# A chunked linear recurrence on TensorE: transposes in place of identity products, one addend moved to VectorE, and a merged product

## What is computed

```python
def wkv7_scan(state, inputs, reverse):
    def step(S, xs):
        r, w, k, v, a, b = xs
        sa = jnp.einsum('bhvk,bhk->bhv', S, a)
        S = S * w[:, :, None, :] + sa[..., None] * b[:, :, None, :] + v[..., None] * k[:, :, None, :]
        return S, jnp.einsum('bhvk,bhk->bhv', S, r)
    ...
# before it:  kk = kk * lax.rsqrt(jnp.sum(jnp.square(kk), -1, keepdims=True) + 1e-12)
# after it:   var = jnp.mean(jnp.square(y - mu), -1, keepdims=True)
#             yn = (y - mu) * lax.rsqrt(var + GN_EPS)
```

## Time and profile before

| | |
|---|---|
| time, median of 3 | 3914.93 us (3911.76 to 3934.26) |
| span of the profiled execution | 3915.0 us |
| TensorE busy | 3610.4 us, 92% |
| VectorE / ScalarE / GpSimd busy | 2019.5 / 1544.0 / 251.1 us |
| mean granted TensorE clock | 0.965 |

### The profile page before, as it was taken

How to read it: one execution, slowest core, us unless ns; L and a number is a source line. 1 busy time by engine, 2 the same in 40 slices (tenths; PEclk the granted TensorE clock), 3 DMA queues, 4 the chain that set the end, 5 groups by cost and what they waited for, 6 DMA issues and landing times. The chain is left out here.

```text
span 3915.0 us, 73945 instructions
## 1 busy us (share of the span) xinstructions
PE 3610.4 (92%) x32796; PEld 2969.4 (76%) x32796; DVE 2019.5 (52%) x3476; ACT 1544.0 (39%) x2599; POOL 251.1 (6%) x295
## 2 busy tenths in 40 slices
PE   7899999999899998989988799989999999999998
PEld 3577666767666676777678689847989799999877
DVE  1444454544445457675465646666544455555444
ACT  1333343333333333354454444334443444444433
POOL 0001111110111113002000000100000000000000
PEclk8899899999999998999999899999999999999999
DMA  9423333242343315443324454424554545555554
GB/s 365 145 74 96 89 106 104 81 126 70 94 126 91 100 56 192 170 153 106 97 97 138 154 166 143 138 97 140 172 183 140 169 163 183 183 179 189 194 174 160
DMA packets 349484, 548.76 MB, mean 140 GB/s; under 512 B 11724, under 2 KB 119916, under 8 KB 346988
## 3 DMA queue, kind: packets, MB, share of 16 engines
q1 hardware_dynamic: 346716, 538.78, 42.6%
q10 hardware_dynamic: 2448, 5.24, 0.4%
HBM read 535.86 MB, written 8.13 MB: 139 GB/s over the span
## 5 line engine op out<-in xcount | busy, mean ns | idle before, releaser
L302 PE MATMUL lane<-r,r 128*128 128x256 f32 (+1 forms) x8520 | 1504.7, 325 | 48.4 <-DVE r L260 41.7
L302 PE MATMUL bank<-r,r 128*128 128x512 f32 (+2 forms) x6360 | 1403.0, 359 | 37.6 <-DVE r L260 29.0
L302 PEld LDWEIGHTS lane<-r,r 128*128 128x128 f32 x8520 | 1260.6, 190 | 222.2 <-DVE r L260 48.6
L260 DVE TENSOR_TENSOR r<-ring,r 128x1024 fp32r<-128x1024 f32 x770 | 939.6, 1227 | 940.9 <-ACT r L299 939.6
L302 PEld LDWEIGHTS bank<-r,r 128*128 128x128 f32 x6360 | 1045.0, 193 | 253.5 <-issue 55.3
L299 ACT ACTIVATE r<-ring 128x1024 fp32r<-128x1024 f32 x770 | 807.9, 1055 | 967.5 <-PE lane L302 566.7
L302 PE MATMUL lane<-arena 64*64 64x64 f32 (+5 forms) x13708 | 664.2, 250 | 57.1 <-issue 20.4
L302 PEld LDWEIGHTS lane<-arena 64*64 64x64 f32 (+3 forms) x13708 | 504.9, 140 | 203.3 <-issue 121.4
L299 ACT ACTIVATE arena<-lane 128x256 f32<-128x256 f32 (+3 forms) x578 | 252.6, 457 | 567.0 <-PE lane L302 468.0
L271 DVE COPY arena<-lane 128x256 f32<-128x256 f32 (+3 forms) x366 | 131.7, 361 | 303.5 <-PE lane L302 300.5
L260 DVE TENSOR_TENSOR arena<-arena 128x256 f32<-128x256 f32 (+7 forms) x568 | 259.8, 488 | 36.0 <-ACT arena L299 14.8
(11 more groups left out here) (95 smaller groups left out, 1357.5 us busy)
## 6 DMA issues: line engine op xcount, KB each, us to landing
ring<-in_w_gate_up SPq DMA_DIRECT2D x88, 1024.0 KB, 5.1
ring<-in_mod_w SPq DMA_DIRECT2D x73, 1024.0 KB, 5.3
ring<-in_ev_w_in SPq DMA_DIRECT2D x44, 1024.0 KB, 8.7
ring<-in_w_down SPq DMA_DIRECT2D x44, 1024.0 KB, 5.1
ring<-in_od_w_in SPq DMA_DIRECT2D x40, 1024.0 KB, 5.1
ring<-in_w_in SPq DMA_DIRECT2D x40, 1024.0 KB, 5.1
ring<-in_w_xkv SPq DMA_DIRECT2D x32, 1024.0 KB, 5.2
ring<-in_ev_w_out SPq DMA_DIRECT2D x28, 1024.0 KB, 5.1
```

The costliest lines, as they stand in the source:

```text
L260: return Nothing() if self.e is None else self.e.tensor_tensor(o, a, b, op)
L302: return Nothing() if self.e is None else self.e.matmul(o, l, r, start=start, stop=stop)
```

## The change

Three things. `spread` uses `pe.tr` in place of `pe.mm` with the same tile and identity. VectorE also writes I + PT for `c` = 1, in two instructions of 64 partitions after the one for `c` = 0, each reading one half and writing the other. And `double` is written anew: step 0 has no products for T at all, and ScalarE then copies only the parts 0 and 2 of its bank; in steps 1 to 3 the products for PT and T of `c` = 1 are one of 128 columns, as those of `c` = 0; the identity product comes after the product with P and not before.

```diff
     def spread(s, b):
         for c in range(2):
-            i = pe.mm(M.bank[b[0]][:, c * P:c * P + P], s.rs[:, c * P:c * P + P], ident, True, True)
+            i = pe.tr(M.bank[b[0]][:, c * P:c * P + P], s.rs[:, c * P:c * P + P], ident)
         i.then_inc(*pe.n(("full", *b)))
...
             four = [(c, q) for c in range(2) for q in range(2)]
-            for q in range(2):
-                pe.mm(out(1, q, 1, 2), C("i64")[half(q), :], tt(1, q), True, False)
+            both = 0 if 1 <= i <= 3 else 1
             for c, q in four:
-                if c == 0 and 1 <= i <= 3:
-                    o = pe.mm(out(c, q, 0, 2), pm(c, q), cur[half(q), c, h, 0:2, :], True, True)
-                elif i or c:
-                    o = pe.mm(out(c, q, 1, 2), pm(c, q), tt(c, q), c == 0, True)
-            if i < 4:
-                for c, q in four[0 if i == 0 else 2:]:
+                if i:
+                    o = pe.mm(out(c, q, both, 2), pm(c, q), cur[half(q), c, h, both:2, :], True, c == 0)
+                else:
                     pe.mm(out(c, q, 0, 1), pm(c, q), pt(c, q), True, True)
+            if i:
+                for q in range(2):
+                    o = pe.mm(out(1, q, 1, 2), C("i64")[half(q), :], cur[half(q), 1, h, 1, :], False, True)
             if i < 5:
                 for c, q in four:
                     o = pe.mm(out(c, q, 2, 3), pt(c, q), pm(c, q), True, True)
...
         v.tt(s.Z[1][:, 0, :, 1, :], s.LR[:, :, 0, 0, :], M.C("i64").unsqueeze(1).to_broadcast([P, 2, 64]), ADD) \
             .then_inc(*v.n(("TT1", d, n)))
+        for q in range(2):
+            at_, to = slice(64 * q, 64 * q + 64), slice(64 - 64 * q, 128 - 64 * q)
+            v.tt(s.Z[1][to, 1, :, 1, :], s.LR[at_, :, 1, 0, :], M.C("i64")[at_, :].unsqueeze(1).to_broadcast([64, 2, 64]), ADD) \
+                .then_inc(*v.n(("TT1_1", d, n)))
...
     def double(d, n, i, bp):
         s = M.lane[d]
-        x = slice(0 if i < 4 else 1, 3 if i < 5 else 2)
+        x = slice(0 if i < 4 else 1, 3 if i < 5 else 2, 1 if i else 2)
```

More of the change, by code:

```diff
@@ L1706, in double @@
             pt = lambda c, q: cur[half(q), c, h, 0, :] if i else s.LR[half(q), h, c, 0, :]
-            tt = lambda c, q: cur[half(q), c, h, 1, :] if i else C("i64")[half(q), :]
             four = [(c, q) for c in range(2) for q in range(2)]
-            for q in range(2):
-                pe.mm(out(1, q, 1, 2), C("i64")[half(q), :], tt(1, q), True, False)
+            both = 0 if 1 <= i <= 3 else 1
             for c, q in four:
-                if c == 0 and 1 <= i <= 3:
-                    o = pe.mm(out(c, q, 0, 2), pm(c, q), cur[half(q), c, h, 0:2, :], True, True)
-                elif i or c:
-                    o = pe.mm(out(c, q, 1, 2), pm(c, q), tt(c, q), c == 0, True)
-            if i < 4:
-                for c, q in four[0 if i == 0 else 2:]:
+                if i:
+                    o = pe.mm(out(c, q, both, 2), pm(c, q), cur[half(q), c, h, both:2, :], True, c == 0)
+                else:
                     pe.mm(out(c, q, 0, 1), pm(c, q), pt(c, q), True, True)
+            if i:
+                for q in range(2):
+                    o = pe.mm(out(1, q, 1, 2), C("i64")[half(q), :], cur[half(q), 1, h, 1, :], False, True)
             if i < 5:
```

## The result

| | before | changed |
|---|---|---|
| median | 3915.58 us (4 runs) | 3890.35 us (4 runs, 3889.63 to 3897.59) |
| profiled execution's span | 3915.0 us | 3895.7 us |
| ratio | | 0.9936 (0.9918 to 0.9954) |

A forecast was written before the change was run, and what follows sets the result against it. TensorE was taken to bound the recurrence, slowed by late weights, late copies and its own instruction fetches. Terms -10.5 + 0 - 7.5 - 2.9 - 14 = -34.9 us gave 3880 us, range 3862 to 3908 (8 in 10).

The forecast's parts named there:

- narrower band: Whole kernel: the forecast's own case, a time of 3870 to 3890 us around 3880; chance 0.45.
- rival (a): Recurrence: instruction fetches don't cause the stalls, or late ones return elsewhere; stalls stay, 3894 us; chance 0.22.
- What bounds, and the fetches: Recurrence: TensorE bounds; doublings wait for its instruction packets, and fewer instructions save 14 us, ends -1.6 and -23.
- The spreads: 64 spreads: four records become two, 14.1 us at most, a quarter lost at weight waits: -10.5 us, ends -5 and -14.
- Step 0: First step of the doublings: c = 1 quarters drop from 16 records to 8, 0.47 us for each of 32 units.
- forward lane's 0 us: Doublings' step 0, forward lane: VectorE's added 0.72 us delays some units, cancelling TensorE's gain: 0 us, ends -5 and +8.
- signs of being wrong: Recurrence: waits stay with fewer packets, idle time before the forward lane's first copy mostly gone, or granted clock under 0.95.
- rival (d): Forward lane: VectorE late in all units, costing 9 us, and fetches catch up without a gain: 3903 us; chance 0.15.
- Steps 1 to 3: Doublings after the first step: merging c = 1 products saves 0.03 us, 96 times: -2.9 us.
- rival (c): Recurrence: transposes leave TensorE at the lower clock more often, mean 0.96 to 0.92, costing 53 us: 3933 us; chance 0.03.
- The part behind the recurrence: After 1495 us: the 2420 us there stay unchanged.
- reverse lane's step 0: Doublings, reverse lane: the copy follows a whole double of the other lane, so 16 x 0.47 = -7.5 us stay.

The follow-up runs named there:

- shifted: Changed kernel with 128 more TensorE instructions in the very first unit, so all later ones stand half a packet further on; ratio to the kernel before 0.9937 (0.9916 to 0.9959).
- unmerged kernel: Changed kernel with the merged product of c = 1 in steps 1 to 3 cut in two of 64 columns again; ratio to the kernel before 0.9977 (0.9963 to 0.9990).
- second profile: Profile from a repeat of the changed kernel, nothing altered; median 3883.23 us against 3911.21 before, ratio 0.9933 (0.9919 to 0.9948).

## Why the prediction was right, and where it was off

The time lies in the range, 0.35 us above the narrower band of 3870 to 3890, and by itself it decides little: it is nearer to rival (a)'s 3894 than to 3880. The waits decide.

- **What bounds, and the fetches** (-14 us, rival (a) against it): right. `<- issue` fell by 14.7 us, 23.2 to 8.5; by (a) it would have stayed. The shifted and the unmerged kernel show that late instruction packets are the cause. I had argued this from a count of packets and four pulses alone. That the size came out within a us is luck: 14 was a choice between 1.6 and 23.
- **The spreads** (-10.5): 11.5 by the steps. The factor is two. The Trainium skill ("TensorE: Matmul & The Clock Gate", Terms) has fp32 transposes four times faster; the six in 0.60 us do not bear that out. The quarter that I took off for weight waits was about right.
- **Step 0**: TensorE saved 13.1 us of the 15 that 0.47 us for each unit make. The **forward lane's 0 us failed**. VectorE is late there as I said, but the term was mis-sized and its wait put at the wrong place. I took 0.21 us for an addition, from one whose next instruction works on the same partitions. The new ones stood 0.32 us apart, and so did the old one ahead of them, since the partitions change each time: 1.5 us ahead of `KR` in place of 0.72. I also priced the delay at the copy of `double` 0, for which `double` 1 waits, while `KV` stands ahead of `double` 1 and waits for `KR`. Of my own signs of being wrong one came true: the idle time before the forward lane's first copy is gone in most units, there in 10 units before and in 2 after. Measured: 11.9 us of waits in the forward lane against 7.0 us saved in its `double` 0, +5 us net in place of 0, still within the ends of -5 and +8. It is half of rival (d), six units with 1.2 to 2.0 us and the others with less than 0.9.
- **Steps 1 to 3** (-2.9): as a price of records it doesn't show. `double` 1 to 5 gave -22.7 us, and the distances at the packets' border in them fell from 31.2 to 8.6, by 22.6. One stall of 4 us moved on to `KV`, so -18.7 stay, where the terms "steps 1 to 3" and "fetches" together were -16.9. The merging pays by the packets that it saves.
- **The clock** (rival (c)): the recurrence stays at 0.96, with 384 transposes in it in place of 256, so the slower end did not come. The rule of the same page of the Trainium skill (Part 4), by which transposes don't count, is not borne out, but hardly tested either: products stand around all these transposes.
- **The part behind the recurrence** I left at 2420 us. In the profiled execution it took 2426 against 2418, at 0.97 against 0.98 of the clock. That is not the change: the kernel before with the two additions has the same code there as the kernel before, and its rows say the same as the changed kernel's:

```profile
1494.00:3920.00 2426.00, 2281.88 (x13748) 1975.34 (x13746) 1348.05 (x1886) 1034.62 (x1487) 100.26 (x115) 0.97 0.47 155
```

So of the 35 us forecast 27 stand in the recurrence of the profiled execution. Against the missing 8 stand the forward lane (5), the reverse lane's step 0 (1.4) and 4.4 in steps for which I had no term, less the 2.8 by which the spreads and `double` 1 to 5 gave more than forecast. In the second profile 41 us stand there, with 24 us less at the lower clock. So chance in the clock is as large as what is missing, and the forward lane is the part of it that an experiment shows: with the additions moved the kernel gains 14 us.

## What to carry to other kernels

Where an engine stands still with no releaser, count its instructions from the start: if the stalls lie a fixed number apart (here 256 or a multiple), the instruction stream is the limit, and a merged or removed instruction is worth more than the time of its columns. When work moves to a neighbour that is idle on average, cost the order on that neighbour's queue, from its instruction to the first wait of the bound engine behind it; here the same two instructions cost 14 us ahead of one instruction of VectorE, and behind it nothing that could be measured. And price an instruction by its distance to the next one, with the partitions of both.

## What the runs showed that I had not expected

**The longest packet waits stand behind bulk transfers.** In each of the 14 traces the two longest stalls, 1.8 to 3.8 us, stand in units 4 and 12. The DMA of the changed kernel from 508 to 524 us, 40 slices of 0.4 us:

```profile
DMA  0000094699999899999999980000000100000000
GB/s 0 0 0 0 0 102 56 184 364 404 410 410 399 302 273 347 335 325 312 330 385 335 371 239 15 9 9 19 1 0 0 41 0 0 0 0 0 0 0 0
```

The transfers run at 300 to 400 GB/s until about 517.5 us. The instruction packet that TensorE needs from 515.48 us on starts at 516.96 us, and TensorE goes on at 519.50, 2.5 us after that start; in the stalls over 0.7 us of the kernel before it is 2.2 to 2.9 us. In the kernel before, the transfers end at 526.4 us, the packet starts at 525.01, and TensorE stands until 527.54. That the transfers hold the packet up is read from this order of events; no run leaves them out.

**VectorE loses 0.10 to 0.11 us at a change of partitions**: additions of 0.28 us are 0.21 apart on the same half and 0.31 to 0.32 apart where the next one reads or writes other partitions (the variant with each addition made twice).

**Where the instructions are removed counts.** Taking step 0's identity products back adds four packets and brings the stalls without a releaser from 8.5 to 10.4 us; taking the merged product apart adds six and brings them to 19.0. My reading, which no run tests: the merged products stand in the run of doublings with no fill between them, where packets can't catch up.
